# Delta levels of a two-block kernel: T, U and X updates on all four 64x64 tiles of the array

## The reference

```python
def gated_delta_chunkwise(q, k, v, g, beta):
    ...
    A = jnp.where(strict, jnp.einsum('bhnid,bhnjd->bhnij', k_beta, kc) * L, 0.0)
    eye = jnp.eye(CHUNK, dtype=f32)
    rhs = jnp.concatenate([vc * bc[..., None], k_beta * jnp.exp(G)[..., None]], axis=-1)
    sol = lax.linalg.triangular_solve(eye + A, rhs, left_side=True, lower=True, unit_diagonal=True)
    u, w = sol[..., :dv], sol[..., dv:]
    ...
```

## Time and profile before

| | |
|---|---|
| median of 3 runs | 2277.95 us (2277.83 to 2278.04) |
| profiled execution, its time | 2278.09 us |
| its span | 2276.4 us |
| PE busy | 2234.2 us, 98% |
| DVE busy | 1067.6 us, 47% |
| ACT busy | 801.5 us, 35% |
| POOL busy | 942.5 us, 41% |

### The profile page before, as it was taken

How to read it: one execution, slowest core, us unless ns; L and a number is a source line. 1 busy time by engine, 2 the same in 40 slices (tenths; PEclk the granted TensorE clock), 3 DMA queues, 4 the chain that set the end, 5 groups by cost and what they waited for, 6 DMA issues and landing times.

```text
span 2276.4 us, 30104 instructions
## 1 busy us (share of the span) xinstructions
PE 2234.2 (98%) x12106; PEld 1804.7 (79%) x12106; DVE 1067.6 (47%) x1508; ACT 801.5 (35%) x825; POOL 942.5 (41%) x509
## 2 busy tenths in 40 slices
PE   7999999999999999999999999999999999999998
PEld 6888888776656888888888788887888878888887
DVE  5423202775853353331054542646556545888701
ACT  4222313447654342222242632332424243322213
POOL 4555544343312445554444244323233343444443
PEclk9999999999999999999999999999999999999999
DMA  4233323343322333223232112212121243233232
GB/s 151 93 92 104 90 93 100 83 77 56 75 99 92 100 106 98 92 83 103 100 103 89 56 61 93 94 56 75 56 75 56 77 147 111 93 92 94 72 101 83
DMA packets 162169, 203.36 MB, mean 89 GB/s; under 512 B 12236, under 2 KB 117015, under 8 KB 162071
## 3 DMA queue, kind: packets, MB, share of 16 engines
q1 hardware_dynamic: 155296, 197.16, 28.6%
q10 hardware_dynamic: 6775, 4.80, 0.7%
HBM read 191.45 MB, written 10.49 MB: 89 GB/s over the span
## 4 chain that ended last, share of the span: by engine, by line
PE 85%; DVE 5%; issue 4%; ACT 3%; POOL 1%; DMA 0%; ACTq 0%; POOLq 0%; DVEq 0%
PE PS L213 23%; PE PS L215 22%; PE PS L214 22%; PE PS L244 2%; PE PS L246 2%; PE PS L245 2%; DVE cv L2327 2%; POOL wl L204 1%; PE PS L1134 1%; PE PS L2138 1%; PE PS L2153 1%; PE PS L2156 1%; PE PS L1674 1%; PE PS L1231 1%; PE PS L1050 0%
## 5 line engine op out<-in xcount | busy, mean ns | idle before, releaser
L204 POOL TENSOR_TENSOR wl<-raw,wh 128x1024 fp32r<-128x1024 f32 x335 | 863.6, 2593 | 1228.5 <-ACT wh L193 1202.8
L213 PE MATMUL PS<-h_hi,wh 128*128 128x512 f32 x1696 | 677.3, 399 | 7.9 <-ACT stage_a L863 3.0
L215 PE MATMUL PS<-h_hi,wl 128*128 128x512 f32 x1696 | 661.9, 390 | 0.0
L214 PE MATMUL PS<-h_lo,wh 128*128 128x512 f32 x1696 | 661.3, 390 | 0.0
L193 ACT ACTIVATE wh<-raw 128x2048 fp32r<-128x2048 f32 (+1 forms) x214 | 332.6, 1554 | 838.0 <-PE PS L215 791.6
L213 PEld LDWEIGHTS PS<-h_hi,wh 128*128 128x128 f32 x1696 | 318.9, 188 | 91.7 <-issue 20.3
L215 PEld LDWEIGHTS PS<-h_hi,wl 128*128 128x128 f32 x1696 | 318.7, 188 | 67.5
L214 PEld LDWEIGHTS PS<-h_lo,wh 128*128 128x128 f32 x1696 | 319.3, 188 | 61.8 <-issue 0.7
L213 PE MATMUL PS<-act_hi,wh 128*128 (+1 forms) x528 | 205.9, 390 | 1.0 <-POOL wl L204 1.0
L215 PE MATMUL PS<-act_hi,wl 128*128 (+1 forms) x528 | 205.4, 389 | 0.0
L214 PE MATMUL PS<-act_lo,wh 128*128 (+1 forms) x528 | 205.4, 389 | 0.0
(11 more groups left out here) (450 smaller groups left out, 2868.1 us busy)
## 6 DMA issues: line engine op xcount, KB each, us to landing
raw<-in_w_in_dram SPq DMA_DIRECT2D x94, 512.0 KB, 4.6
raw<-in_w_up_dram SPq DMA_DIRECT2D x82, 512.0 KB, 4.6
raw<-in_w_down_dram SPq DMA_DIRECT2D x132, 256.0 KB, 2.7
raw<-in_w_gate_dram SPq DMA_DIRECT2D x42, 512.0 KB, 3.8
raw<-in_w_in_dram SPq DMA_DIRECT2D x20, 256.0 KB, 3.6
raw<-in_w_out_dram SPq DMA_DIRECT2D x16, 256.0 KB, 2.8
raw<-in_w_ret_br_dram SPq DMA_DIRECT2D x8, 512.0 KB, 4.1
gates<-stage SPq DMA_DIRECT2D x16, 256.0 KB, 5.5
```

The source lines that it names most:

```text
L204: ins = nc.gpsimd.tensor_tensor(wl[:, slot, part], raw[:, slot, part], wh[:, slot, part].bitcast(F32), ALU.subtract)
L213: nc.tensor.matmul(dst, sh, mh, start=start, stop=False)
L214: nc.tensor.matmul(dst, sh, ml, start=False, stop=False)
L215: return nc.tensor.matmul(dst, sl, mh, start=False, stop=stop)
```

## The change

U's blocks and X's masked blocks move to the other half of the partitions: what belongs to the block of T in partitions r now lies in partitions 64 - r (`other`). So X is a product with rows r and columns 64 - r, T's update has rows 64 - r and columns r, and U's update has rows and columns 64 - r. X and T's update are off-diagonal tiles, U's update a diagonal one.

T and U of one head get a bank each. The banks 4, 5 and 6, 7 take turns by level: X of level l has one pair, T and U of head 0 the other pair, T and U of head 1 the pair of X. The start block of `Uc` is written across the halves, ACT reads it back across them, and the last two products use partitions 0 to 63. The number and the order of the instructions are the same on all engines (6188 rows on PE in both, with counts joined).

```diff
+    def block_of_X(e, c, r):
+        return wX[r:r + 64, e, c * 64:(c + 1) * 64]
+
+    def other(r):
+
+        return 64 - r
+
+    def pair_of(l):
+        return (4, 5) if l % 2 == 0 else (6, 7)
+
+    def x_bank(l, e):
+        return pair_of(l)[e]
+
+    def tu_banks(l, e):
+
+        return pair_of(l + 1) if e == 0 else pair_of(l)
+
+    def last_bank(e):
+        return pair_of(len(LEVELS) + 1)[e]
...
                     for c in range(NT):
                         for r in (0, 64):
-                            ins = mm(PS[r:r + 64, 4 + e, c * 64:(c + 1) * 64], quarter(wAT, e, c, r, r), block_of(Tc, e, c, r),
-                                     start=True, stop=True)
+                            o = other(r)
+                            ins = mm(PS[o:o + 64, x_bank(l, e), c * 64:(c + 1) * 64], quarter(wAT, e, c, r, r),
+                                     block_of(Tc, e, c, r), start=True, stop=True)
                     ins.then_inc(d_X, 1)
...
                     pe.wait_ge(d_Xm, n + e + 1)
+                    t_bank, u_bank = tu_banks(l, e)
                     for c in range(NT):
-                        lo, hi = c * 32, (c + 1) * 32
+                        part = slice(c * 32, (c + 1) * 32)
                         for r in (0, 64):
-                            mm(PS[r:r + 64, 6 + e, lo:hi], block_of(Uc, e, c, r), halves(wX[r:r + 64, e, c * 64:(c + 1) * 64], b)[0],
+                            o = other(r)
+                            mm(PS[r:r + 64, t_bank, part], block_of(Uc, e, c, o), halves(block_of_X(e, c, o), b)[0],
                                start=True, stop=True)
-                        for r in (0, 64):
-                            ins = mm(PS[r:r + 64, 6 + e, 128 + lo:128 + hi], wX[r:r + 64, e, c * 64:(c + 1) * 64],
-                                     halves(block_of(Uc, e, c, r), b)[1], start=True, stop=True)
+                        for o in (0, 64):
+                            ins = mm(PS[o:o + 64, u_bank, part], block_of_X(e, c, o), halves(block_of(Uc, e, c, o), b)[1],
+                                     start=True, stop=True)
                     ins.then_inc(d_TU, 1)
...
-                    ins = mm(PS[64:P, 4 + e, c * 64:(c + 1) * 64], quarter(wAT, e, c, 0, 64), block_of(Tc, e, c, 0),
-                             start=True, stop=True)
+                    ins = mm(PS[0:64, x_bank(len(LEVELS), e), c * 64:(c + 1) * 64], quarter(wAT, e, c, 0, 64),
+                             block_of(Tc, e, c, 0), start=True, stop=True)
...
-                    ins = mm(PS[0:64, 6 + e, c * 64:(c + 1) * 64], wX[64:P, e, c * 64:(c + 1) * 64], block_of(Uc, e, c, 64),
+                    ins = mm(PS[0:64, last_bank(e), c * 64:(c + 1) * 64], block_of_X(e, c, 0), block_of(Uc, e, c, other(64)),
                              start=True, stop=True)
...
-                ins = act.activation(quarters(wU, r, r), blocks(Uc[r:r + 64, :]), ACT.Copy)
+                ins = act.activation(quarters(wU, r, r), blocks(Uc[other(r):other(r) + 64, :]), ACT.Copy)
...
-            def start_block(dst, src, mask):
+            def start_block(dst, src, mask, half):
 
                 for r in (0, 64):
-                    ins = tt(blocks(dst[r:r + 64, :]), quarters(src, r, r),
+                    o = half(r)
+                    ins = tt(blocks(dst[o:o + 64, :]), quarters(src, r, r),
                              mask[r:r + 64, 0:64].unsqueeze(1).to_broadcast([64, 2 * NT, 64]), ALU.mult)
...
-            at_point(start_block(Uc, wAT[:, :, :], level1T), "dve")
+            at_point(start_block(Uc, wAT[:, :, :], level1T, other), "dve")
...
-                    tt(first, first, PS[:, 6 + e, 0:128].rearrange("p (g r) -> p g r", r=b), ALU.subtract)
-                    tt(second, second, PS[:, 6 + e, 128:256].rearrange("p (g r) -> p g r", r=b), ALU.subtract).then_inc(d_Um, 1)
+                    t_bank, u_bank = tu_banks(l, e)
+                    tt(first, first, PS[:, t_bank, 0:128].rearrange("p (g r) -> p g r", r=b), ALU.subtract)
+                    tt(second, second, PS[:, u_bank, 0:128].rearrange("p (g r) -> p g r", r=b), ALU.subtract).then_inc(d_Um, 1)
```

More of the change, by code:

```diff
@@ L2387, in delta_dve @@
                 tap()
-            start_block(Tc, wU, level[1])
+            start_block(Tc, wU, level[1], lambda r: r)
             await_point(dve, "act", pp, "AT")
-            at_point(start_block(Uc, wAT[:, :, :], level1T), "dve")
+            at_point(start_block(Uc, wAT[:, :, :], level1T, other), "dve")
             dve.memset(quarters(wU, 64, 0), 0.0)
@@ L2401, in delta_dve @@
                     mask = level[b][:, 0:64].unsqueeze(1).to_broadcast([P, NT, 64])
-                    tt(blocks(wX[:, e, 0:256]), blocks(PS[:, 4 + e, 0:256]), mask, ALU.mult).then_inc(d_Xm, 1)
+                    tt(blocks(wX[:, e, 0:256]), blocks(PS[:, x_bank(l, e), 0:256]), mask, ALU.mult).then_inc(d_Xm, 1)
                 if l == 0:
@@ L2414, in delta_dve @@
                 dve.wait_ge(d_X, n + e + 1)
-                dve.tensor_scalar(wX[64:P, e, 0:256], PS[64:P, 4 + e, 0:256], -1.0, None, ALU.mult).then_inc(d_Xm, 1)
+                dve.tensor_scalar(wX[0:64, e, 0:256], PS[0:64, x_bank(len(LEVELS), e), 0:256], -1.0, None,
+                                  ALU.mult).then_inc(d_Xm, 1)
             for e in range(2):
@@ L2418, in delta_dve @@
                 dve.tensor_copy(wU[0:64, e, :].rearrange("p (c j) -> p c j", c=NT)[:, :, 64:P],
-                                blocks(PS[0:64, 6 + e, 0:256])).then_inc(d_Um, 1)
+                                blocks(PS[0:64, last_bank(e), 0:256])).then_inc(d_Um, 1)
             for c in range(NT):
```

## The result

| | before | changed |
|---|---|---|
| median of the runs | 2276.83 us (2276.2 to 2278.04, 12 runs) | 2282.98 us (2280.58 to 2284.65, 12 runs) |
| profiled execution | 2278.09 us | 2283.54 us |
| its span | 2276.4 us | 2281.8 us |

The 12 runs of before take in the three that stand ahead of the prediction. The ratio is 1.0025, with an interval of 1.0017 to 1.0032: the changed kernel is slower by a quarter of a per cent, where 15 us less were forecast. In the changed file X stands at L2159, T's update at L2176, U's at L2179, the transposes of the third level at L2167, the masks at L2426, the scores at L2428 and L2429, the subtractions at L2435 and L2436, the start blocks at L2404 and L2407.

A forecast was written before the change was run, and what follows sets the result against it. PE, busy 98% of the span, was taken to bound the kernel. 4 x (4 x 0.92 + 0.11) = 15.2 us off the profiled 2278.1 gives 2262.9, the median 0.14 lower: 2262.8 us, range 2261.3 to 2270.5.

The forecast's parts named there:

- A run saves 0.92 us: PE's run of T and U updates in each level: four tiles overlap fully, so 1.98 us becomes 1.06.
- Rival 1: T and U runs on PE: tiles sharing rows or columns take turns, nothing gained, 2278 us; chance 0.07.
- Rival 2: T and U runs: PE's feed becomes the limit, at 22 ns a pass saving 0.44 us a run, 2270.5 us; chance 0.08.
- Rival 3: T and U runs: PE drains between row tiles writing the same partitions, slower, 2342 us at 0.20 a change; chance 0.04.
- The gain is whole in levels 2 to 5: DVE's subtractions end before X needs them in these levels, so each keeps the run's full 0.92 us.
- The cover: Slack between the end of DVE's subtractions and the next X: 0.77 us for head 0, 0.76 for head 1.
- a new wait of PE in level 1: X would wait some 0.7 us for DVE's subtractions, behind its two scores operations.
- Level 1 saves 0.11 us: DVE's scores operations delay its subtractions, so X can start at 1459.19 at the earliest, where it started at 1459.30.
- No difference for DVE across the halves: Uc's start block, written to the other 64 partitions than it reads, would still take 1.38 us on DVE.
- Rival 4: Full overlap, but crossing halves costs DVE, up to 2268.4 us; chance inside the 0.81 of full overlap.
- The sum: Four head pairs, each with four levels saving 0.92 us and one saving 0.11: 15.2 us less.

The follow-up runs named there:

- e1: Changed kernel, with POOL's second weight unit waiting until DVE's two operations on the scores are done: 2263.7 us, ratio 0.9941.
- e11: Kernel before, with the two multiplications of Uc's start block in the other order, partitions 64 to 127 first: 2300.05 us, ratio 1.0087.
- e10: Changed kernel, with three one-column ACT copies ahead of the rounding that releases POOL's second unit, no new wait: 2264.17 us, ratio 0.9936.
- e6: Kernel before, with one one-column memset on DVE right ahead of its first scores operation in level 1: 2278.03 us, ratio 1.001.
- e7: Changed kernel, with one one-column ACT copy ahead of the rounding that releases POOL's second unit: 2269.88 us, ratio 0.9967.
- e8: e1 with all T updates of a head first, then all its U updates, same tiles and banks: 2268.26 us, ratio 0.9958.
- e3: Changed kernel, with DVE's memset of wU moved from ahead of level 1 to behind level 4: 2282.39 us, ratio 1.0015.
- e9: Kernel before, with eight one-column memsets on DVE right ahead of its first scores operation in level 1: 2301.33 us, ratio 1.0098.
- e12: Changed kernel, with Uc's start block writing partitions 0 to 63 first, each multiplication still reading the other half: 2281.43 us, ratio 1.0015.
- e4: Changed kernel, with two filler products moved from behind the levels to level 1 in the first three head pairs: 2268.0 us, ratio 0.9964.

## Why the prediction was wrong, point by point

- *A run saves 0.92 us.* Right: 1.98 to 1.07, and 3.93 us from X to X where 3.92 was forecast. Rivals 1, 2 and 3 are refuted by this. 64 passes start 14.5 ns apart and keep that up, and the loads of tiles on the same rows lie over each other. The rule and the floor of some 25 ns from the Trainium skill ("TensorE: Matmul & The Clock Gate", Part 3 and Back-to-back issue gap) don't hold for these 64x64 tiles: by the one the run would have stayed at 1.98 us, by the other its 64 passes alone would have taken 1.6, where they took 0.93.
- *The gain is whole in levels 2 to 5.* The cover was right. The group of all X in the changed kernel (busy, mean ns | idle before it, and who ended it) shows it:

```profile
L2159 PE MATMUL PS<-work,w_AT 64*64 64x64 f32 x640 | 26.2, 240 | 14.7 <-DVE work L2436 12.0 <-ACT stage L1545 2.8
```

  Of the 12.0 us that X waited for DVE, 4 x 2.98 = 11.9 lie in level 1, and nothing to speak of in the others. But it was taken that PE's clock is a constant, because the earlier trace rows have 1.00. This is the second step that failed: the prediction foresaw a new wait of PE in level 1 and gave it no price in clock. Levels 2 and 3 lost 2.96 us a head pair to it. The wait that was foreseen, some 0.7 us, would have been harmless: in e1 it is 0.86 us and the clock stays.
- *Level 1 saves 0.11 us.* This is the first step that failed. L2404 was read with its 1.22 us, as a price that moves along with DVE. It "waits for nothing of the run", which is true, but its row held only as long as it started ahead of POOL. The earlier trace rows show neither POOL nor how close it was. A look at POOL in the same microsecond would have shown two starts at 1456.27, and L2394 with 1.61 us for 128x8 elements would have shown what becomes of the second. Level 1 lost 2.13 us instead.
- *No difference for DVE across the halves,* with 1.38 to 2.76 us as bounds. The multiplications do take what they took, 1.39 us. The cost is 0.09 us in the start of the first one, a size that I would have left out as nothing. It went through POOL's earlier unit to DVE's L2394, and decided who came first in level 1 (e11). Rival 4 named the right edit and a wrong mechanism, and its bound, 2268.4 us, was far too low, for it let DVE's delay cost PE its own length and no more.
- *The sum.* Forecast per head pair: -3.8 us. Measured: 4 x -0.92 + 2.13 + 2.96 = +1.4 us, which is 5.6 us in four; the profiled execution was 5.4 us longer. With the order of DVE and POOL put right (e10), the sum of the prediction comes out: 2264.2 us for 2262.8, the rest being level 1 at 4.85 and not 4.74 us (the 0.09 us again) and the gaps without a cause.

The Trainium skill has the mechanism ("SBUF — State Buffer", Who interferes with whom): VectorE with two SBUF inputs and a GpSimd operation that reads SBUF share a port pair, the first to start keeps it for its whole instruction, and the order of issue, not the shape, decides who is blocked. The traces agree, but for the ties of e6 and e7, where POOL's recorded start is 6 to 8 ns ahead and DVE still goes first: when first, DVE's operation takes 1.22 us and POOL's 3.46; when second, DVE's takes 3.35, to 1.08 us after the end of POOL's, which then takes 2.38.

## What to carry to other kernels

Before a duration is carried over to a changed kernel, see what another engine does at its start: where DVE and POOL start within 0.1 us of each other, the order of the two is part of what either row shows, and a delay too small to appear in a sum can turn it round. Here a wait that fixes the order, as in e1, kept the gain made on PE. And a wait on the engine that sets the end has a second price, the granted clock after it, which here was larger (2.96 us) than the wait's own lengthening (2.13 us).

## What the runs showed of the hardware

- Four 64x64 fp32 tiles side by side start a pass every 14.5 ns on average, kept up for 64 passes. PE starts matmuls ahead of earlier ones of the program: two passes of U after ten of T, where 16 of T stand first (e8).
- DVE keeps its turn with POOL's recorded start up to 8 ns ahead and loses it with 17 (e6, e7).
- With a wait of PE of 2.0 to 3.1 us in level 1 the granted clock fell to 1.2 GHz in every such head pair of the changed kernel, e3, e7, e9, e11 and e12: at the earliest 1.4 us before PE resumed (e12), at the latest 1.65 us after (e3), and for 3.4 to 13.7 us. It did not fall with 1.61 us, nor once with 2.98 us (e4).
- A DVE operation of 64 partitions starts 0.61 us after a 128-partition one of 0.69 us if it reads and writes partitions 0 to 63, and 0.70 us after it otherwise (e11, e12).
